# Mixers' end of a two-layer decoder step: one more weight block split, raw weight slots shifted, two blocks' halves made earlier, and a one-column square root ahead of the norms' square roots

## What is computed

```
proj = x @ w_in                                   # 23 blocks of 128 output columns
hgrn2 heads, retention heads, S5 groups           # the three mixers
o_hg = o_hg * rsqrt(mean(o_hg^2) + eps) * w * silu(g)
o_rt = (o_rt - mu) * rsqrt(var + eps) * w * silu(g)
mixed = concat(o_hg, o_rt, y5) @ w_out            # 8 blocks
x = layer_norm(ALPHA * x + mixed)
x = layer_norm(ALPHA * x + relu(x @ w_up)^2 @ w_down)
```

## Time and profile before

| what | value |
|---|---|
| median of 3 runs | 764.63 us (762.09, 765.79, 764.63) |
| profiled execution, its own time | 763.1 us |
| its span in the profile | 761.3 us, mean granted TensorE clock 0.985 |
| TensorE busy | 718.5 us (94%), 7142 matmul records |
| VectorE busy | 532.4 us (70%) |
| ScalarE busy | 396.2 us (52%) |
| weight transfers | 190 of 512 KB |

### The profile page before, as it was taken

How to read it: one execution, slowest core, us unless ns; L and a number is a source line. 1 busy time by engine, 2 the same in 40 slices (tenths; PEclk the granted TensorE clock), 3 DMA queues, 4 the chain that set the end, 5 groups by cost and what they waited for, 6 DMA issues and landing times.

```text
span 761.3 us, 17305 instructions
## 1 busy us (share of the span) xinstructions
PE 718.5 (94%) x7142; PEld 662.9 (87%) x7142; DVE 532.4 (70%) x959; ACT 396.2 (52%) x752; POOL 42.3 (6%) x58
## 2 busy tenths in 40 slices
PE   5989899989999999999969899999999999999994
PEld 4877768769999999999969797877899999999993
DVE  7996884377787987963775987435768876655474
ACT  4514034455687556774448223334648865577342
POOL 5000012100000000000030001020000000000001
PEclk9999999999999999999989999999999999999997
DMA  8531213545454655554524312331635555555531
GB/s 342 210 111 37 80 60 122 219 132 173 131 178 164 195 192 175 186 169 139 175 76 139 91 52 85 129 111 65 221 111 195 184 177 182 179 190 173 189 114 58
DMA packets 30718, 112.50 MB, mean 148 GB/s; under 512 B 3536, under 2 KB 3744, under 8 KB 30256
## 3 DMA queue, kind: packets, MB, share of 16 engines
q1 hardware_dynamic: 28080, 100.78, 40.0%
q0 software_dynamic: 1984, 9.54, 3.2%
q10 hardware_dynamic: 576, 1.08, 0.4%
HBM read 107.20 MB, written 4.18 MB: 146 GB/s over the span
## 4 chain that ended last, share of the span: by engine, by line
PE 74%; DVE 9%; ACT 2%; issue 1%; DMA 1%; DVEq 0%; ACTq 0%
PE stream L1043 19%; PE stream L1044 18%; PE stream L1045 18%; PE stream L1018 8%; PE mix L948 2%; DVE w_low L1559 1%; DMA w_raw<-in_weights 1%; PE mix L766 1%; PE mix L839 1%; PE mix L689 1%; ACT w_high L1102 1%; PE mix L799 1%; PE mix L897 0%; PE mix L811 0%; DVE scratch L1891 0%
## 5 line engine op out<-in xcount | busy, mean ns | idle before, releaser
L1559 DVE TENSOR_TENSOR w_low<-w_raw,w_high 128x1024 fp32r<-128x1024 f32 x153 | 187.3, 1224 | 106.3 <-ACT w_high L1102 104.9
L1102 ACT ACTIVATE w_high<-w_raw 128x1024 fp32r<-128x1024 f32 x153 | 162.0, 1059 | 144.8 <-PE stream L1045 131.6
L1043 PE MATMUL stream<-h_high,w_high 128*128 128x264 f32 x512 | 146.4, 286 | 0.0
L1045 PE MATMUL stream<-h_high,w_low 128*128 128x264 f32 x512 | 145.1, 283 | 0.0
L1044 PE MATMUL stream<-h_low,w_high 128*128 128x264 f32 x512 | 145.0, 283 | 0.0
L1043 PE MATMUL stream<-a_high,w_high 128*128 128x264 f32 x456 | 134.0, 294 | 9.1 <-DVE a_low L2145 6.3
L1018 PE MATMUL stream<-X,w_raw 128*128 128x264 f32 x528 | 129.6, 398 | 10.3 <-DMA w_raw<-in_weights 8.2
L1044 PE MATMUL stream<-a_low,w_high 128*128 128x264 f32 x456 | 130.5, 286 | 0.0
L1045 PE MATMUL stream<-a_high,w_low 128*128 128x264 f32 x456 | 130.2, 286 | 0.0
L1018 PEld LDWEIGHTS stream<-X,w_raw 128*128 128x128 f32 x528 | 99.6, 194 | 32.2 <-DMA w_raw<-in_weights 8.6
L1043 PEld LDWEIGHTS stream<-a_high,w_high 128*128 128x128 f32 x456 | 87.0, 191 | 12.0 <-issue 11.0
(11 more groups left out here) (382 smaller groups left out, 994.1 us busy)
## 6 DMA issues: line engine op xcount, KB each, us to landing
w_raw<-in_weights SPq DMA_DIRECT2D x190, 512.0 KB, 3.5
mats<-in_matrices POOLq DMA_DIRECT2D x2, 1024.0 KB, 6.0
S_hg<-in_state_hg POOLq DMA_DIRECT2D x2, 768.0 KB, 7.5
out_hg_s<-S_hg POOLq DMA_DIRECT2D x2, 768.0 KB, 3.7
consts<-in_constants POOLq DMA_DIRECT2D x1, 1499.5 KB, 9.5
X<-in_xT ACTq DMA_DIRECT2D x4, 264.0 KB, 4.9
out_y<-X SPq DMA_DIRECT2D x4, 264.0 KB, 2.1
S_rt<-in_state_rt POOLq DMA_DIRECT2D x2, 512.0 KB, 8.7
```

Source lines behind the costliest of these rows:

```text
L1043: pe.matmul(bnk[:, 0:width], wh, xh, start=(first and kk == 0), stop=False)
L1045: mm = pe.matmul(bnk[:, 0:width], wl, xh, start=False, stop=(last and kk == 7))
L1102: act.activation(w_high[:, n % SPLIT_SLOTS, :], w_raw[:, n % RAW_SLOTS, :], ACT.Copy).then_inc(high_ready, 1)
L1559: put(tt(w_low[:, n % SPLIT_SLOTS, :], w_raw[:, n % RAW_SLOTS, :], w_high[:, n % SPLIT_SLOTS, :].bitcast(F32), ALU.subtract), low_ready)
```

## The change

Four things, in both layers.

1. Block 22 is split (it was not in either layer).
2. The raw slots are given by a table, `RAW_SLOT`, instead of n mod 3; from block 26 on in each layer they are shifted by two. So block 26 takes the slot of block 25, block 27 that of 23 and block 28 that of 24. `RAW_PREV[n]` is the former block in the slot. Before, 25, 26, 27 and 28 followed 22, 23, 24 and 25. The halves' slots (`SPLIT_SLOT`, `SPLIT_PREV`) are now counted over the split blocks alone.
3. The halves of blocks 25 and 26 (`EARLY`) are made at fixed places: those of block 25 at step 22 ahead of that step's mixer work, on both engines; the high half of 26 between the fifth and the sixth high half of `MIX` in `mixer_end`, its low half behind the last low half there.
4. `head_root` begins with a root of one column of a constant, and step `DOWN_B` + 10 of layer 0 has one too, so that the table load stands ahead of these and not ahead of the root proper.

```diff
-UNSPLIT = (tuple(_c for _c in range(OUT0 + 2) if _c != RG + 1), tuple(range(12, OUT0 + 2)))
+UNSPLIT = (tuple(_c for _c in range(OUT0 + 2) if _c not in (RG + 1, RG + 2)), tuple(_c for _c in range(12, OUT0 + 2) if _c != RG + 2))
...
+for _n in range(DEPTH * N_CHUNKS):
+    if _n % N_CHUNKS == OUT0 + 3:
+        _shift += 2
+    _slot = (_n + _shift) % RAW_SLOTS
+    RAW_SLOT.append(_slot)
+    RAW_PREV.append(_last.get(_slot))
...
+EARLY = (OUT0 + 2, OUT0 + 3)
...
-            return RAW_SLOTS <= n < DEPTH * N_CHUNKS and not SPLIT[n - RAW_SLOTS]
+            return n < DEPTH * N_CHUNKS and n % N_CHUNKS < OUT0 + 2 and RAW_PREV[n] is not None and not SPLIT[RAW_PREV[n]]
+
+        def split_ahead(n):
+
+            return n % N_CHUNKS not in EARLY and not split_late(n)
...
-                if n >= RAW_SLOTS:
-                    wait_raw_read(sp, n - RAW_SLOTS)
-                sp.dma_start(w_raw[:, n % RAW_SLOTS, :], weights[n // N_CHUNKS, n % N_CHUNKS]).then_inc(raw_loaded[n % RAW_SLOTS], 16)
+                if RAW_PREV[n] is not None:
+                    wait_raw_read(sp, RAW_PREV[n])
+                sp.dma_start(w_raw[:, RAW_SLOT[n], :], weights[n // N_CHUNKS, n % N_CHUNKS]).then_inc(raw_loaded[RAW_SLOT[n]], 16)
...
             def head_root(l, name, w, ready):
 
+                act.activation(head_sd[96:128, w, 0:1], cv("eps")[96:128], ACT.Sqrt)
                 b, fu = got(l, name)
...
                 for i in (0, 1, 2):
                     split_a(l, i, hmix_ready, 3 * l + i + 1)
+                split_high(l * N_CHUNKS + EARLY[1])
                 for i in range(3, 6):
                     split_a(l, i, rmix_ready, 3 * l + i - 2)
...
+                if k == 10 and l + 1 < DEPTH:
+                    act.activation(row_sums[:, 0, 0:1], cv("eps"), ACT.Sqrt)
...
                     if split_late(n + 1):
                         split_high(n + 1)
-                    if not split_late(n + AHEAD):
+                    if split_ahead(n + AHEAD):
                         split_high(n + AHEAD)
+                    if c == N_IN - 1:
+                        split_high(l * N_CHUNKS + EARLY[0])
                     if c < N_IN:
                         mixer_work(l, c)
...
                 for k in range(2, KT):
                     split_a(l, 1, k, MIX, MIX_ORDER[k])
+                split_low(l * N_CHUNKS + EARLY[1])
```

More of the change, by code:

```diff
@@ L172 @@
 MIX_BANKS = 4
-UNSPLIT = (tuple(_c for _c in range(OUT0 + 2) if _c != RG + 1), tuple(range(12, OUT0 + 2)))
+UNSPLIT = (tuple(_c for _c in range(OUT0 + 2) if _c not in (RG + 1, RG + 2)), tuple(_c for _c in range(12, OUT0 + 2) if _c != RG + 2))
 SPLIT = [_n % N_CHUNKS not in UNSPLIT[_n // N_CHUNKS] for _n in range(DEPTH * N_CHUNKS)]
+RAW_SLOT, RAW_TURN, RAW_PREV = [], [], []
+_last, _turns = {}, {}
+_shift = 0
+for _n in range(DEPTH * N_CHUNKS):
[4 more added lines that the diff above has]
+    RAW_PREV.append(_last.get(_slot))
+    _turns[_slot] = _turns.get(_slot, 0) + 1
+    RAW_TURN.append(_turns[_slot])
+    _last[_slot] = _n
+SPLIT_BLOCKS = [_n for _n in range(DEPTH * N_CHUNKS) if SPLIT[_n]]
+SPLIT_SLOT = {_n: _i % SPLIT_SLOTS for _i, _n in enumerate(SPLIT_BLOCKS)}
+SPLIT_PREV = {_n: SPLIT_BLOCKS[_i - SPLIT_SLOTS] if _i >= SPLIT_SLOTS else None for _i, _n in enumerate(SPLIT_BLOCKS)}
+EARLY = (OUT0 + 2, OUT0 + 3)
 FIRST_SPLIT = [min(_c for _c in range(N_CHUNKS) if _c not in UNSPLIT[_l]) for _l in range(DEPTH)]
@@ L1017, in dense @@
                         x = MIX if c >= OUT0 else X
-                        mm = pe.matmul(bnk[:, 0:T], w_raw[:, n % RAW_SLOTS, 128 * k:128 * k + 128], x[:, k, :], start=(kk == 0), stop=(kk == 7))
+                        mm = pe.matmul(bnk[:, 0:T], w_raw[:, RAW_SLOT[n], 128 * k:128 * k + 128], x[:, k, :], start=(kk == 0), stop=(kk == 7))
                     if kks[-1] == 7:
```

16 lines of the change are left out of this document (9 added, 7 removed).

## The result

The changed kernel takes 768.77 us, median of 19 runs (763.6 to 773.88); the kernel before takes 764.79 us beside it (19 runs, 761.86 to 767.82). The ratio is 1.0047, 95% interval 1.0031 to 1.0063: **3.6 us slower, between 2.4 and 4.8 us**. That is inside the range that was predicted (761.5 to 769.0), but near its upper end, three times the size forecast (+1.2 us), and just under the 0.5% that the prediction took as the line between "same" and "slower". One of the 26 runs of the kernel before that stand beside the experiments with block 22's and 21's changes took 1196.76 us at a granted clock of 0.55; it is left out everywhere.

What follows compares the result with a forecast made beforehand. TensorE, 74% of the chain that ended last, was taken as the bound, so the change counts only where it waits. Layer 0's -2.8 plus layer 1's +4.0 gave +1.2 us, median 765.8 us; range 761.5 to 769.0.

Steps and rivals of the forecast that it cites:

- Block 25's halves, layer 0: Before block 25 in layer 0: raw 25 lands at 144 to 145.5, cost 0, TensorE's 1.43 us wait goes.
- The root, layer 0: At `ret_var` in layer 0: root ready about 1.6 us earlier, VectorE late next, 0.4 us gained, bounds 0 to 0.52.
- Block 31, layer 0: Two TensorE waits in block 31, layer 0, 1.01 us together, go as transfers leave earlier: 1.0 us gained, bounds 0 to 1.0.
- Rival (d): Layer 0: the slot change does not clear the backlog, block 31's waits stay, +1.0, 766.8 us; chance 0.06.
- Block 25's halves, layer 1: Layer 1: raw 25 lands about 522.0, ScalarE's list waits, first `ret_mu` 4.7 us later; layer +4.0 us, bounds +2.3 to +5.5.
- block 22's halves: Layer 1: the high half holds VectorE's state products up by about 2 us, at cost 0, bounds 0 and 0.3.
- The clock: Layer 1's `ret_mu` wait: granted clock falls to 0.50 at about 523, rises about 528; +4.0 us, +3.1 if it stays up.
- rival (a): Layer 1: the clock stays up in the wait, sum +0.3, 764.9 us; chance 0.18.
- (c): Layer 1: the clock stays down after 3.7 us of work, until about 533.5; +4.0, 768.6 us; chance 0.08.
- wrong if the clock falls in layer 0: Sign set beforehand: a fall of the granted clock in layer 0 would show the forecast wrong; no size given.
- Rival (b): Layer 1 is not held up because raw 25 lands before it matters; -4.7, 759.9 us; chance 0.08.
- The seam: Between the layers: TensorE's 6.27 us idle unchanged; hidden table load at the norm gains 0, bounds 0 and -0.1.

Runs made afterwards that it cites:

- both moved again: Second sample of the changed kernel with layer 1's block 25 halves later and block 22 halves behind step 21's mixer work: 760.21 us, 0.9924 of the kernel before.
- 25 later: Changed kernel with block 25's two early halves in layer 1 moved behind the work leading to the root: 761.29 us, ratio 0.9947 to the kernel before.
- Both moved: Changed kernel with layer 1's block 25 halves later and block 22 halves behind step 21's mixer work, first sample: 758.84 us, 0.9913 of the kernel before.

## Why the prediction was right or wrong

The time fell in the range, and the mechanism in layer 1 was the one forecast; two terms were mis-sized, in the same direction.

- **Block 25's halves, layer 0: right.** Landing at 148.3 us, with the front 3.4 us later, is 144.9 on the prediction's clock (144 to 145.5). No wait before block 25. Over the eleven traces with layer 0 changed the landing came at 144.2 to 146.9 on that clock, wider than the bounds; at 146.4 (both moved again) the stretch was 0.2 us longer, at 146.9 (25 later) TensorE waited 0.7 us. "Cost 0" held in nine of eleven.
- **The root, layer 0: right.** Forecast -0.4, and VectorE next in line; the roots alone gave 0.33, and the reciprocal follows the product without idling. The stretch as a whole gained 1.99 us where 1.8 was forecast.
- **Block 31, layer 0: the step that failed, -1.0.** "I take the whole 1.0" blamed the slot for a landing. With the order of before and an earlier landing the waits were gone (two traces of three); with the new slots they came back in small (0.3 and 0.4 us, two traces of eleven). The term stood in the sum at its full size because the one profiled execution happened to have the waits. Up to the seam the old order took 226.6, 226.8 and 228.2 us, the new one 226.6 in nine traces and 227.2 and 227.3 in two, so the slots may be worth a few tenths of a microsecond in the mean; that is not shown. Rival (d) has the right place, but not its reason. Layer 0 is worth -2.0 us, not -2.8.
- **Block 25's halves, layer 1: right in mechanism, too small by 1.4 us.** Forecast +4.0 (its own times give +3.9: 534.8 - 529.47 - 1.43), measured +5.4 (+4.4 in one execution), inside its bounds of +2.3 to +5.5. Of the 1.4: 0.57 us is "cost 0, bounds 0 and 0.3" for block 22's halves, which TensorE paid with the wait in `ret_o` and behind it (moving them gave back 0.77 in the experiment); 0.36 is the landing: the first `ret_mu` came 31.52 us behind the cut at block 18 where 30.59 was forecast, 0.93 later, and 0.57 of that is block 22's; 0.47 is what follows `ret_mu`, nearly all the clock: forecast 0.9 us, measured 1.3.
- **The clock: right in kind, too short.** It was down during the wait, but up again only 5.0 us after TensorE resumed, where 3.4 to 3.7 was taken from the seam; with the clock held up, the same way was 1.3 us shorter, against the 0.9 forecast. Neither rival (a) nor (c) happened. The sign "wrong if the clock falls in layer 0" was badly put: it fell in layer 0's front in both kernels (at 94 us before, at 107 us changed). Rival (b) needs raw 25 before the sigmoid of block 21; splitting block 21 makes exactly that, and the stretch is then 3 us under before.
- **The seam: right.** 6.27 us, gain 0. An estimate by the Trainium skill, "ScalarE: Activation LUTs", section "What ACT_TABLE_LOAD costs", had given 1.1 us there. The traces disagree: the one-column root starts at 158.92, when the load that began at 157.63 has lasted its 1.28 us, and the norm gained nothing. By an estimate from the Trainium skill, "DMA: Bandwidth & Descriptors", section "Bandwidth" (1 MB in 6.15 us from GpSimd), raw 25 would have landed at 524.4. The pair issued at 518.27 was there at 523.24, after 4.97 us, longer than the 4.1 us of the earlier trace rows and still shorter than 6.15.
- **The sum.** -2.8 + 4.0 = +1.2 should have been -2.0 + 5.4 = +3.4, and +3.6 was measured. The range held because it took in rival (c) at 768.6, another mechanism of the same size: that is luck. Its "-1.2 to +1.5" does not follow from the terms' bounds. These add up to between -0.7 and +3.7, which is -1.9 and +2.5 around the forecast, and layer 0's small end is -1.4 and not -1.8 when the root gives nothing. The chance of 0.10 for slower was small for that, as the time came out at +3.6.

"Both moved" is timed 2.4 us (first sample) and 1.8 us (second) faster than its stretches say. The traced executions do not explain it, as their fronts are long. The other runs do in part: each has a span and a mean granted clock on record, and its span times one minus the clock is what it lost to the clock. The runs of both moved lost 11.4 and 11.8 us in the mean, those of the kernel before beside them 12.4 and 13.2. Without the clock the means differ by 4.8 and 4.2 us, near the stretches' 4.3 and 4.0.

## What to carry to other kernels

Before an operation that waits for a transfer is put ahead of others in an engine's list, ask what frees the transfer's buffer: here ScalarE stood 9.3 us behind data that could not leave sooner, and moving two instructions behind the work that did not need them was worth 7.6 us. An edit that gains in one version can lose in another, when it delays what frees a buffer that the other version fills early. And a short wait in one profile is a property of the kernel only if a second profile has it: the same order of work gave 0 and 1.0 us in block 31.
